# First factors of both scan directions ahead of the key and query masks, and GpSimd's later level masks held back

## The reference

```python
def step(S, inp):
    r_t, w_t, k_t, v_t, a_t, b_t = inp
    sa = jnp.einsum('zbhvk,zbhk->zbhv', S, a_t)
    S = S * w_t[..., None, :] + sa[..., :, None] * b_t[..., None, :] + v_t[..., :, None] * k_t[..., None, :]
    return S, jnp.einsum('zbhvk,zbhk->zbhv', S, r_t)

xs = (shared(r), time_major(decay), time_major(k_dir), shared(v), shared(-kk), time_major(b_dir))
_, ys = lax.scan(step, jnp.zeros((2, B, H, N, N), f32), xs)
ys = ys.transpose(1, 2, 0, 3, 4)
y = ys[0] + ys[1][:, ::-1]
```

## Time and profile before

| | |
|---|---|
| median of 3 runs | 1379.88 us (1375.46 to 1380.42) |
| the profiled execution, its own time | 1380.09 us |
| its span, first to last instruction | 1378.2 us |
| TensorE busy | 1309.7 us, 95% of the span |
| VectorE busy | 924.2 us, 67% |
| ScalarE busy | 646.7 us, 47% |
| GpSimd busy | 443.5 us, 32% |
| chain that ended last, by engine | TensorE 79%, VectorE 14%, ScalarE 4%, issue 2% |
| mean granted clock of TensorE | 0.961 of full speed |

### The profile page before, as it was taken

How to read it: one execution, slowest core, us unless ns; L and a number is a source line. 1 busy time by engine, 2 the same in 40 slices (tenths; PEclk the granted TensorE clock), 3 DMA queues, 4 the chain that set the end, 5 groups by cost and what they waited for, 6 DMA issues and landing times.

```text
span 1378.2 us, 32598 instructions
## 1 busy us (share of the span) xinstructions
PE 1309.7 (95%) x13824; PEld 1189.7 (86%) x13824; DVE 924.2 (67%) x1270; ACT 646.7 (47%) x1045; POOL 443.5 (32%) x220
## 2 busy tenths in 40 slices
PE   7999999999899999999997898999999999899998
PEld 5899998878799998899996888999888988789998
DVE  7777666886766656766678966455655535777775
ACT  5544546553645456444444666233333322644443
POOL 1344442111344443344441002333333312344442
PEclk9999999999999999999998999599999989999999
DMA  8355555322455555455554340010000012455553
GB/s 325 138 183 183 183 188 181 135 92 100 176 183 183 186 186 219 151 185 189 188 190 153 138 156 29 2 49 3 4 3 4 3 49 93 183 183 183 183 183 122
DMA packets 18674, 188.31 MB, mean 137 GB/s; under 512 B 2064, under 2 KB 2576, under 8 KB 3600
## 3 DMA queue, kind: packets, MB, share of 16 engines
q1 hardware_dynamic: 18576, 186.84, 37.5%
HBM read 185.78 MB, written 1.05 MB: 136 GB/s over the span
## 4 chain that ended last, share of the span: by engine, by line
PE 79%; DVE 14%; ACT 4%; issue 2%; DMA 0%; SPq 0%; DVEq 0%; ACTq 0%
PE gu_bank L257 21%; PE gu_bank L259 11%; PE gu_bank L1399 8%; PE bank L236 7%; PE bank L237 6%; PE bank L238 6%; PE bank L1380 6%; PE gu_bank L236 3%; PE gu_bank L238 2%; PE gu_bank L237 2%; DVE WL L193 2%; PE gu_bank L1380 2%; ACT WH L186 1%; DVE XSQ L407 1%; DVE HX L383 1%
## 5 line engine op out<-in xcount | busy, mean ns | idle before, releaser
L202 POOL TENSOR_TENSOR WL<-raw,WH 128x1024 fp32r<-128x1024 f32 x102 | 341.7, 3350 | 599.3 <-ACT WH L187 577.8
L257 PE MATMUL gu_bank<-HX,WH 128*128 128x512 f32 x1408 | 508.5, 403 | 14.5 <-DVE WL L193 11.7
L259 PE MATMUL gu_bank<-HX,WL 128*128 128x256 f32 x1408 | 397.6, 282 | 0.0
L193 DVE TENSOR_TENSOR WL<-raw,WH 128x2048 fp32r<-128x2048 f32 (+1 forms) x114 | 252.6, 2216 | 138.3 <-ACT WH L186 138.2
L257 PEld LDWEIGHTS gu_bank<-HX,WH 128*128 128x128 f32 x1408 | 267.3, 190 | 80.3 <-DVE WL L193 9.3
L259 PEld LDWEIGHTS gu_bank<-HX,WL 128*128 128x128 f32 x1408 | 268.9, 191 | 0.2
L186 ACT ACTIVATE WH<-raw 128x2048 fp32r<-128x2048 f32 (+1 forms) x114 | 204.6, 1795 | 23.3 <-PE gu_bank L238 13.5
L236 PE MATMUL bank<-PH,WH 128*128 128x256 f32 (+1 forms) x720 | 201.9, 284 | 1.0 <-ACT arena L1882 1.0
L237 PE MATMUL bank<-PL,WH 128*128 128x256 f32 (+1 forms) x720 | 201.9, 284 | 0.0
L238 PE MATMUL bank<-PH,WL 128*128 128x256 f32 (+1 forms) x720 | 201.8, 284 | 0.0
L438 ACT ACTIVATE work<-work 128x256 f32<-128x256 f32 x88 | 36.8, 418 | 277.7 <-DVE work L490 277.7
(11 more groups left out here) (307 smaller groups left out, 2125.4 us busy)
## 6 DMA issues: line engine op xcount, KB each, us to landing
raw<-stream_in SPq DMA_DIRECT2D x114, 1536.0 KB, 6.4
cst<-const_in SPq DMA_DIRECT2D x1, 1568.0 KB, 17.3
X<-xT_in SPq DMA_DIRECT2D x1, 1024.0 KB, 5.7
raw<-stream_in SPq DMA_DIRECT2D x1, 1024.0 KB, 7.8
arena<-hconst_in SPq DMA_DIRECT2D x2, 512.0 KB, 11.0
out<-X SPq DMA_DIRECT2D x4, 256.0 KB, 2.4
arena<-hconst_in SPq DMA_DIRECT2D x1, 768.0 KB, 14.1
arena<-fw_in SPq DMA_DIRECT2D x1, 512.0 KB, 8.5
```

The lines of the kernel that those rows point to most:

```text
L193: nc.vector.tensor_tensor(WL[:, slot, :cut], raw[:, slot, :cut], WH[:, slot, :cut].bitcast(fp32), ALU.subtract).then_inc(lo_ready, 1)
L202: (eng or nc.gpsimd).tensor_tensor(WL[:, slot, cut:end], raw[:, slot, cut:end], WH[:, slot, cut:end].bitcast(fp32), ALU.subtract).then_inc ...
L257: nc.tensor.matmul(out[:, :], WH[:, slot, w:w + P], HX[:, x, :, :].rearrange("p i t -> p (i t)"), start=k == 0, stop=False)
L259: return nc.tensor.matmul(out[:, L:2 * L], WL[:, slot, w:w + P], HH[:, x, :], start=False, stop=k == CT - 1)
```

## The change

In `dve_tile` the loop over the directions is split. First both directions' first-factor masks are made (L1736 before, L1737 after), then for each direction the mask of `ABD` and the sum with the identity, then the copy for the chunk step, and only then both key masks into `AQ` (L1747 after) and the query masks. Since the key masks now read `DBANK` later, a new semaphore `aq_read` is counted by them, and TensorE waits for it ahead of the level-0 products that write over `DBANK`. In `pool_tile` GpSimd waits ahead of the masks of level 1 until both directions' `t_ready` is there.

```diff
@@ dve_tile
             for z in range(2):
                 dve.wait_ge(aq_done, 2 * t + z + 1)
-                aq = units_of(DBANK[z])
                 if t:
                     dve.wait_ge(qf_ready, 2 * t + z - 1)
-                own(tt(TQ[:, z, 1], aq[:, :, 0:CH], mask64("first_incl", z * P), ALU.mult))
-                own(tt(AQ[p][:, z * NCH:(z + 1) * NCH, :], aq[:, :, CH:P], mask64("first_incl", z * P + CH), ALU.mult))
+                own(tt(TQ[:, z, 1], units_of(DBANK[z])[:, :, 0:CH], mask64("first_incl", z * P), ALU.mult))
+            for z in range(2):
                 dve.wait_ge(abd_ready, 2 * t + z + 1)
                 own(tt(TQ[:, z, 0], ABD[:, z], mask64("first", z * CH), ALU.mult))
                 own.settle()
@@
             if chunks:
                 dve_rc(dve, t - 1, 0)
+            for z in range(2):
+                tt(AQ[p][:, z * NCH:(z + 1) * NCH, :], units_of(DBANK[z])[:, :, CH:P], mask64("first_incl", z * P + CH),
+                   ALU.mult).then_inc(aq_read, 1)
             for z in range(2):
                 dve.wait_ge(bq_done, 2 * t + z + 1)
@@ pe_tile, level loop
                 for z in range(2):
                     pe.wait_ge(zb_ready, 10 * t + 2 * n + z + 1)
+                    if n == 0:
+                        pe.wait_ge(aq_read, 2 * t + z + 1)
@@ pool_tile
                     if n == 0:
                         pool.wait_ge(abd_ready, 2 * t + z + 1)
+                    elif n == 1:
+                        pool.wait_ge(t_ready, 12 * t + 2)
```

More of the change, by code:

```diff
@@ L1244, in build @@
         tr_done, tr_ready, a_done, a_ready = sem("tr_done"), sem("tr_ready"), sem("a_done"), sem("a_ready")
-        aq_done, bq_done, abd_ready = sem("aq_done"), sem("bq_done"), sem("abd_ready")
+        aq_done, aq_read, bq_done, abd_ready = sem("aq_done"), sem("aq_read"), sem("bq_done"), sem("abd_ready")
         xl_ready, z_done, zb_ready, d_done, t_ready = (sem(n) for n in "xl_ready z_done zb_ready d_done t_ready".split())
```

## The result

| | before | after |
|---|---|---|
| median | 1377.67 us of 4 runs (1374.90 to 1380.42) | 1360.88 us of 4 runs (1359.35 to 1364.55) |
| profiled execution, its own time | 1380.09 us | 1364.55 us |
| its span | 1378.2 us | 1362.6 us |
| mean granted clock of TensorE | 0.961 | 0.975 |

The ratio is 0.9882, with a 95% interval of 0.9849 to 0.9915. In the changed kernel L1740 is the mask of `ABD`, L1743 the sum with the identity, L1747 the key masks, L1751 the query masks, L1656 the scans, L1708 and L1712 the copies, L1764 the level sums.

The account below looks back on a forecast made before the run. TensorE was taken to carry most of the chain, so time is won only where it stalls or runs slowly. 7.3 (clock) + 0.7 (pair 0) + 6 x 0.0 = 8.0 us off 1380.1, giving 1372 us; range 1363 to 1378.

Parts of the forecast that it names:

- The front: VectorE's second sum, no longer behind a GpSimd mask, ends 1.09 us earlier; TensorE's stall falls from 1.97 to 0.88.
- The transposes: TensorE's transposes wait for the query masks, now behind both key masks; this gives back 0.43 us a pair.
- The scans: VectorE's prefix scans meet GpSimd's held masks and take turns, giving back 0.7 us; second-step stall 1.2 us.
- A pair at the upper clock: Gains and give-backs within one head pair cancel: 0.0 us gained, distance staying 32.5 us.
- The clock in pairs 2, 4, 5 and 6: With no 2.0 us stalls left, these pairs lose their low-clock stretches: 7.3 us gained.
- I leave it low: Pair 0, with narrow products throughout, stays at the lower clock and gains only 1.09 - 0.43 = 0.7 us.
- The side remark: In pair 0 VectorE's prefix comes after GpSimd's masks are done, so nothing is given back there.
- Rival B: More than the sum: scans not caught, or pair 0 partly at the upper clock; 1361 to 1368 us, chance 0.16.
- A: The clock falls as before in the slow pairs: 3.5 us gained, 1376.6 us; chance 0.27.
- C: Slower: masks catch four prefix instructions, second-step stall reaches 2.0 us, clock falls; 1386 us in the middle, chance 0.07.
- D: Direction 1's second sum still meets a GpSimd mask; front gains 0.6 us, mostly taken back; 1379 us, chance 0.06.

Follow-up runs that it names:

- e2: The changed kernel without GpSimd's wait, VectorE's new order kept: 1372.56 us, ratio 0.9973 to the kernel before.
- e6: As e3, with direction 1's key mask moved behind the query masks: 1356.79 us, ratio 0.9869 to the kernel before.
- e3: The changed kernel with GpSimd's masks of level 3 and on held until VectorE's prefix sums are done: 1360.81 us, ratio 0.9883 to the kernel before.
- b2: The kernel before, unchanged, run again for a second trace: 1375.85 us, ratio 1.0000.
- b3: The kernel before, unchanged, a third trace from a single execution: 1369.44 us.
- a2: The changed kernel, unchanged, run again for a second trace: 1364.39 us, ratio 0.9911 to the kernel before.
- a4: The changed kernel, unchanged, a fourth trace from a single execution: 1368.13 us.
- e1: The kernel before with GpSimd's wait alone, VectorE's order the old one: 1371.63 us, ratio 0.9961 to the kernel before.

## Why the prediction was right and wrong, point by point

- **The front.** Forecast 0.67 for the second sum and a stall of 0.88; measured 0.69 and 0.87 to 0.88. The hold does it: without it (e2) the sum takes 1.09 again.
- **The transposes.** Forecast 0.43 given back. TensorE comes to them 924.53 - 922.41 = 2.12 us behind the second sum, against 969.96 - 968.18 = 1.78 in the earlier trace rows: 0.34. e6 takes 0.27 of it back.
- **The scans.** Whether they take turns with GpSimd was the open question; I took the turn-taking with 0.7 us, by L1739 as the nearest row. Measured 0.91 and 1.14, a stall of 1.25 (forecast 1.2), and 0.72 us by e3. What the prediction cites of the Trainium skill, page "SBUF — State Buffer", section "Who interferes with whom", held for the scans.
- **A pair at the upper clock.** Forecast 32.5 to 32.5; measured 32.50 to 32.47. Three terms cancelled as worked out: 1.09 gained at the front, 0.43 and 0.69 given back in the forecast, 0.34 and 0.72 in the traces.
- **The clock in pairs 2, 4, 5 and 6.** Forecast 7.3 us; in the profiled pair of executions 169.8 to 162.5, 7.3. Over four executions each it is 170.2 to 163.5, 6.6, since falls come back in some. The size was right, and the match to a tenth is luck of the two traces: b2 and b3 have a fall in all five pairs, a2 and a4 in two. The reason given, that only stalls of 2.0 us are followed by a fall, was not: that bound was read from one execution, and 1.28 us brings back nearly all of them. Pair 1, my evidence that 1.44 is harmless, is only so in the executions where pair 0 ran low to its end; in b2 and b3, with stalls of 1.74 and 2.02, it has a low stretch of 6.8 us that starts behind the first of them.
- **The step that failed: "I leave it low", pair 0 at 0.7 us.** Measured 11.1 in the first two traces, 7.1 in the mean over four each (34.3 to 27.2). By these means the distances gained 13.3 us instead of 8.0: 6.4 more in pair 0, 0.7 less in pairs 2 to 6, and 0.4 lost in pair 1, where nothing was forecast. I took a 34 us low stretch as a property of narrow products, where it began behind a stall that the change halves, and in two of four executions of before it isn't there at all. In equal shares of the two histories the gains of 8 and 3 us would average 5.5, an estimate, so a part of the 7.1 can be the draw. The side remark, that in pair 0 the prefix comes after GpSimd is done, failed with it: at the upper level the scans of pair 0 met the masks too, with 0.90 and 1.15 us. Rival B named this very case, with a chance of 0.16 and a price of 4 to 8 us on the whole; with pair 0's 3.1 or 11.1 us in place of 0.7, the same sum gives 10.4 to 18.4 us, 1362 to 1370.
- **Rivals A, C, D.** A came in as a part: 4 of 20 pairs fell again, at 0.4 to 1.8 us each. C did not: in pairs 2 to 6 the masks caught the two scans and nothing behind them, and the second stall ended at 1.25, short of the 1.45 where I put its point; e1 shows that it was near, with 1.58 and three falls. D is excluded by the 0.69.

What stays open: which history ahead of pair 0 an execution gets, and why the same stall of 0.88 is followed by a fall in one pair and not in the next. Whether the moment of a stall counts beside its length, no run here separates. Two things in the traces speak for it: pair 0 above, with the fall 0.4 or 1.9 us behind the same stall, and falls that come at even steps, 34.1 us apart in b2 from pair 2 to pair 6 and 68.3 apart in e1, in every second pair. The parts also do not add up to the whole (4.7 and 4.3, 4.1 and 3.2 against about 12); that this is one pair's stretch moving the next ones was argued, not shown.

## What to carry to other kernels

Where TensorE is the bound and its granted clock drops behind short stalls, price a change by the stall that it shortens and by the low stretch that may follow: here 0.4 us more per pair cost 9 us in the whole, 3 of them by length. A clock pattern that stands in one profiled execution is one draw, so read the distances of repeated stages in several executions before a term or a bound is taken from it. And when a slower engine's work is moved off one instruction, look up which one it meets next: the held masks cost 0.7 us a pair at the scans, and holding them once more took that off the pair at the upper clock, while the 3.6 us by which the median fell are not clear of the noise.

## What the runs showed of the hardware that was not expected

- The clock falls behind stalls well under 2 us: in 9 of 10 pairs at 1.28 us, in 11 of 35 at 0.88. In pairs 0 to 6 the low stretches are 3.4 or 6.8 us long, but two executions of before had one of 34 us, in pair 0, where TensorE, at the lower level, was busy for 33.42 of 33.90 us. At the upper level, in the changed kernel, pair 0 is done in 27.2 us, with TensorE busy for 22.22 of 27.00.
- The same program has different low stretches from execution to execution, at the same stalls (30.3 or 38.4 us in pair 0). The Trainium skill, page "TensorE: Matmul & The Clock Gate", Part 1, says that the gate's observation of activity runs free of the kernel, so that the same kernel changes level at different points from run to run. The traces agree as far as these distances go.
- TENSOR_TENSOR_SCAN of VectorE takes turns with GpSimd's masks as an ordinary TENSOR_TENSOR with two inputs in SBUF does: 0.68 and 0.67 us free, 0.91 and 1.14, or 1.25 and 1.14, when caught. A 0.42 us mask behind a 3.52 us weight split took 1.92.
